# Gate and up projections of two swiglus: seven products of halves for 18 of 22 pairs, with the second projection's rows between them

## The reference

```python
def swiglu(x, w_in, w_out):
    gate, up = jnp.split(x @ w_in, 2, axis=-1)
    return (jax.nn.silu(gate) * up) @ w_out
```

## Time and profile before

| | |
|---|---|
| runs, median | 1790.06 us (1788.73 to 1791.06) |
| the profiled execution, its own time | 1788.67 us |
| its span | 1786.9 us |
| granted TensorE clock, mean | 0.998 |
| matmuls | 8634 |
| busy, DVE / ACT / POOL | 879.1 / 676.5 / 9.0 us |
| loaded and stored | 176.85 MB, 99 GB/s |

### The profile page before, as it was taken

How to read it: one execution, slowest core, us unless ns; L and a number is a source line. 1 busy time by engine, 2 the same in 40 slices (tenths; PEclk the granted TensorE clock), 3 DMA queues, 4 the chain that set the end, 5 groups by cost and what they waited for, 6 DMA issues and landing times.

```text
span 1786.9 us, 21356 instructions
## 1 busy us (share of the span) xinstructions
PE 1771.8 (99%) x8634; PEld 1450.8 (81%) x8634; DVE 879.1 (49%) x1440; ACT 676.5 (38%) x1129; POOL 9.0 (1%) x36
## 2 busy tenths in 40 slices
PE   9999999999999999999999999999999999999998
PEld 8777778888888897666888888888888898888887
DVE  4688783333333734555833332338436762434344
ACT  4467633222223234565332231232545552323141
POOL 0000000000000000000000000000000000000000
PEclk9999999999999999999999999999999999999999
DMA  8232223323333342322233333352323333232321
GB/s 289 85 100 85 85 82 98 114 83 95 106 94 106 107 130 72 94 83 60 83 101 100 94 111 83 101 152 76 94 60 103 98 107 106 85 104 94 100 90 47
DMA packets 218180, 176.85 MB, mean 99 GB/s; under 512 B 9010, under 2 KB 177875, under 8 KB 218083
## 3 DMA queue, kind: packets, MB, share of 16 engines
q1 hardware_dynamic: 218082, 175.49, 32.6%
HBM read 173.32 MB, written 7.38 MB: 101 GB/s over the span
## 4 chain that ended last, share of the span: by engine, by line
PE 96%; DVE 3%; DMA 0%; ACT 0%; issue 0%; SPq 0%; DVEq 0%; ACTq 0%
PE ps L577 29%; PE ps L579 29%; PE ps L578 29%; PE ps L857 2%; PE ps L899 1%; PE ps L923 1%; PE ps L911 1%; PE ps L877 1%; PE ps L782 1%; PE ps L867 0%; DVE small L1465 0%; DMA raw<-in_a_w_qkv 0%; DVE xl L1385 0%; DVE x L1527 0%; DVE x L1461 0%; PE ps L887 0%
## 5 line engine op out<-in xcount | busy, mean ns | idle before, releaser
L577 PE MATMUL ps<-xh,whi 128*128 128x512 f32 (+1 forms) x1176 | 442.8, 377 | 0.3 <-DVE xl L1385 0.3
L579 PE MATMUL ps<-xh,wlo 128*128 128x512 f32 (+1 forms) x1176 | 431.6, 367 | 0.0
L578 PE MATMUL ps<-xl,whi 128*128 128x512 f32 (+1 forms) x1176 | 431.1, 367 | 0.0
L1372 DVE TENSOR_TENSOR wlo<-raw,whi 128x1024 fp32r<-128x1024 f32 x235 | 283.4, 1224 | 241.0 <-ACT whi L1067 240.3
L1067 ACT ACTIVATE whi<-raw 128x1024 fp32r<-128x1024 f32 x235 | 243.7, 1050 | 109.9 <-PE ps L579 79.3
L577 PEld LDWEIGHTS ps<-xh,whi 128*128 128x128 f32 x1176 | 222.4, 189 | 46.1 <-issue 10.2
L577 PE MATMUL ps<-whi,hh 128*128 128x512 f32 x648 | 256.8, 396 | 0.8 <-ACT arena L1249 0.8
L579 PE MATMUL ps<-whi,hl 128*128 128x512 f32 x648 | 252.5, 390 | 0.0
L578 PE MATMUL ps<-wlo,hh 128*128 128x512 f32 x648 | 252.2, 389 | 0.0
L579 PEld LDWEIGHTS ps<-xh,wlo 128*128 128x128 f32 x1176 | 222.3, 189 | 36.8
L578 PEld LDWEIGHTS ps<-xl,whi 128*128 128x128 f32 x1176 | 222.5, 189 | 35.8 <-issue 1.2
(11 more groups left out here) (204 smaller groups left out, 2040.9 us busy)
## 6 DMA issues: line engine op xcount, KB each, us to landing
raw<-in_ffn_w_in SPq DMA_DIRECT2D x88, 512.0 KB, 4.1
raw<-in_w_ff SPq DMA_DIRECT2D x64, 512.0 KB, 4.1
raw<-in_ffn_w_out SPq DMA_DIRECT2D x44, 512.0 KB, 3.8
raw<-in_a_w_qkv SPq DMA_DIRECT2D x23, 512.0 KB, 5.0
raw<-in_w_in SPq DMA_DIRECT2D x20, 512.0 KB, 3.8
raw<-in_kv_w SPq DMA_DIRECT2D x16, 512.0 KB, 4.3
bias_skewed<-bias_rows SPq DMA_DIRECT2D x8, 640.0 KB
raw<-in_a_w_o SPq DMA_DIRECT2D x8, 512.0 KB, 4.4
```

Source lines behind the costliest of these rows:

```text
L577: e.matmul(o, ah, bh, start=start, stop=False)
L578: e.matmul(o, ah, bl, start=False, stop=False)
L579: return e.matmul(o, al, bh, start=False, stop=stop)
L1372: e.tensor_tensor(lo, self.raw[:, m % RAW, :], f32(hi), ALU.subtract).then_inc(s.lo, 1)
```

## The change

The first 4 blocks of each swiglu stay as they are. For the other 18, the 1024 features and the 512 tokens are cut into halves, and gate and up are the two halves of the output. Instead of eight products of a half (4 feature blocks, 256 tokens), seven are made, from sums of the weights' halves and of the tokens' halves (Strassen's scheme in Winograd's form). A product is 4 x 3 matmuls of 256 columns.

- Weights: of a pair's two tiles, four unit tiles are made, x1 (up as it is, products 1 and 2), x2 (both sums s2 and s1, products 6 and 5), s4 (half a tile, product 3) and x3 (s3 and the second half of gate, products 7 and 4). DVE makes the four sums of 128 x 512 (`sums`); units are split as tiles are, and SP reloads a raw slot behind the split of s4 or x3.
- Tokens: behind norms 1 and 3 ACT also copies the unrounded tokens out of PSUM (`x_raw`), and during the four plain pairs DVE makes four sums of 128 x 1024, each of which is split.
- Results: products 1, 6, 7 and 4 add up in one PSUM bank, and ACT copies out the state after 1, 6 and 7 (`keep`); 2 stands alone in a second bank, which 5 and 3 then take. DVE adds copies and second bank (`combine`, `hidden`), ACT's silu is in two halves of 256 (`gates`).
- Order: `PIECES` says, for each pair, which of four places between its seven products take a piece of the second projection's rows. There are 56 such pieces, those of blocks 0 to 13; the rows of the last 8 blocks stay at the norm's edge. The groups are 4, 4, 4, 2 and 8 blocks, so DVE adds to `x` 40 times instead of 24.
- Splits run 3 units ahead in the pairs, with one after each product.
- Some semaphores of small loads are merged, so that their users wait for all loads of a set: `a_in` stands for those of the first attention (cosines, sines, masks, gains), `mix_in` counts 112 instead of 80 and takes in the mixer's norm vectors. SP loads norm 4's vectors, and POOL clears the mixer's small tiles, only after the last low part of the second swiglu's hidden blocks.

```diff
-FFN_GROUPS = [(0, 6), (6, 8), (14, 8)]
...
+FFN_GROUPS = [(0, 4), (4, 4), (8, 4), (12, 2), (14, 8)]
+PLAIN = 4
...
+AHEAD_PAIRS = 3
+PUMP = 1
+PIECES = "1011 1011 1011 1011 1011 1111 1111 1111 1111 1111 1111 1111 1111 1011 0101 0101 0101 0101 0000".split()
...
+    def sum_next(self):
+
+        n = self.n_split
+        if n > self.summed and n < len(self.kinds) and self.kinds[n] == "s2":
+            for i in range(3):
+                self.step("sums", n + i)
+            self.summed = n + 2
...
+        if norm in (1, 3) and t == 3:
+            self.t_steps = [("t_sum", 1), ("t_sum", 2), ("t_sum", 3), ("t_split", 1), ("t_sum", 4), ("t_split", 4),
+                            ("t_split", 3), ("t_split", 2)]
...
+    def product(self, pair, j):
+        if self.unfinished:
+            self.step("hidden_low", self.unfinished.pop())
+        name, f = f"ffn_w_in{pair.layer}", pair.f
+        if j == 1:
+            pair.bank1 = self.bank(hold=True)
+            x1 = self.take("cols", name, FF + f * 128, frees=False)
+            pair.units[1], pair.units[2] = (x1, 0), (x1, 1)
+            pair.up = len(self.tiles) - 1
+        elif j == 2:
+            pair.bank2 = self.bank(hold=True)
+        elif j == 6:
+            self.tiles.append(("cols", name, f * 128))
+            pair.gate = len(self.tiles) - 1
+            x2 = self.unit("s2", pair, None)
+            pair.units[6], pair.units[5] = (x2, 0), (x2, 1)
+            pair.units[3] = self.unit("s4", pair, pair.up), 0
+            x3 = self.unit("s3", pair, pair.gate)
+            pair.units[7], pair.units[4] = (x3, 0), (x3, 1)
+        value = pair.done[j] = self.count("product") + 1
+        self.step("product", pair, j)
+        if j in (1, 6, 7):
+            pair.copied[j] = self.count("copied") + 1
+            pair.free[j] = self.read.get((j, pair.buf if j == 6 else 0), 0)
+            self.step("keep", pair, j)
+        if j in (2, 7, 3):
+            pair.combined[j] = self.count("combined") + 1
+            self.read[{2: (1, 0), 7: (7, 0), 3: (6, pair.buf)}[j]] = pair.combined[j]
+            if j != 3:
+                self.step("combine", pair, j, self.counts["h"] - (j == 7))
+        if j in (2, 5, 4, 3):
+            self.done(pair.units[j][0], "product", value)
+        if j == 4:
+            self.release(pair.bank1)
+            pair.gates = self.count("gates") + 1
+            self.step("gates", pair, self.counts["h"])
+        if j == 3:
+            self.release(pair.bank2)
+            pair.hidden = self.block(pair.block)
+            self.count("combined")
+            self.step("hidden", pair)
+            self.unfinished.append(pair)
+        if not self.by_hand:
+            self.pump(PUMP)
+
+    def some_t(self, n):
+
+        for _ in range(min(n, len(self.t_steps))):
+            what, i = self.t_steps.pop(0)
+            if what == "t_sum":
...
+        self.unfinished, self.t_steps = [], []
+        wanted = []
...
+        self.some_t(8)
+        rows = [self.rows("res", (f"ffn_w_out{layer}", 0), f0, nf, norm=norm if f0 == 14 else None, group=g)
+                for g, (f0, nf) in enumerate(FFN_GROUPS)]
+        pieces = itertools.chain(*rows[:-1])
+        pairs = {f: Pair(layer, f) for f in range(PLAIN, 22)}
+        self.ahead = AHEAD_PAIRS
+        for j in (1, 2):
+            self.product(pairs[PLAIN], j)
+        for f in range(PLAIN, 23):
+            here, last, following = pairs.get(f), pairs.get(f - 1), pairs.get(f + 1)
+            n = PIECES[f - PLAIN]
+            for pair, j in ((here, 6), ("rows", 0), (last, 4), (last, 3), ("rows", 1), (here, 5), (following, 1),
+                            ("rows", 2), (here, 7), (following, 2), ("rows", 3)):
+                if pair == "rows":
+                    self.some(pieces, int(n[j]))
+                elif pair:
+                    self.product(pair, j)
+        self.ahead = AHEAD
+        self.step("hidden_low", self.unfinished.pop())
+        assert next(pieces, None) is None
+        self.ffn_blocks[layer] = self.counts["h"]
...
+        self.run(rows[-1])
...
+            elif what == "product":
+                pair, j = arg
+                unit, half = pair.units[j]
+                wh, wl = (part.rearrange("p (k c) -> p k c", k=8) for part in self.parts(unit))
+                w.wait_ge(s.lo, unit + 1)
+                w.wait_ge(s.xl, x_at + 8)
+                if j in (1, 2, 3):
+                    c, k0 = slice(256, 512) if j == 3 else slice(0, 256), 0 if j == 1 else 4
+                    th, tl = (v[:, k0:k0 + 4, c] for v in (xh, xl))
+                else:
+                    w.wait_ge(s.t_lo, t_at + {5: 1, 4: 2, 7: 3, 6: 4}[j])
+                    th, tl = self.t[{4: 4, 5: 1, 6: 2, 7: 3}[j]]
+                b = pair.bank1 if j in (1, 6, 7, 4) else pair.bank2
+                if j in (1, 2):
+                    w.wait_ge(*freed[b])
+                elif j in (5, 3):
+                    w.wait_ge(s.combined, pair.combined[2 if j == 5 else 7])
+                else:
+                    w.wait_ge(s.copied, pair.copied[{6: 1, 7: 6, 4: 7}[j]])
+                for k in range(4):
+                    m = mm3(e, ps[b][:, 0:256], wh[:, 4 * half + k, :], wl[:, 4 * half + k, :], th[:, k, :],
+                            tl[:, k, :], j in (1, 2, 5) and k == 0, k == 3, skip_group_check=True)
+                m.then_inc(s.product, 1)
...
+                w.wait_ge(s.product, pair.done[j])
+                if pair.free[j]:
+                    w.wait_ge(s.combined, pair.free[j])
+                e.activation(dst, ps[pair.bank1][:, 0:256], ACT.Copy).then_inc(s.copied, 1)
+
+            elif what == "gates":
+                pair, blocks = arg
+                w.wait_ge(s.product, pair.done[4])
+                w.wait_ge(s.hl, blocks - 1)
+                e.activation(self.silu_out[pair.buf][:, 0:256], ps[pair.bank1][:, 0:256], ACT.Silu).then_inc(s.act, 1)
+                own += 1
+                w.wait_ge(s.combined, pair.combined[7])
+                out = self.silu_out[pair.buf][:, 256:512]
+                e.activation(out, out, ACT.Silu).then_inc(s.gates, 1)
+
+            elif what == "hidden":
+                pair, = arg
+                w.wait_ge(s.combined, pair.combined[3] + 1)
+                e.activation(self.hh[:, pair.block, :], self.h_out[pair.buf], ACT.Copy).then_inc(s.hh, 1)
+
+            elif what == "t_split":
+                i, n = arg
+                w.wait_ge(s.t_raw, n if i == 1 else (n + 3) // 4 * 4)
+                if i == 2:
...
+                    if norm in (1, 3):
+                        e.activation(self.x_raw[:, half * 4:half * 4 + 4, t * 128:t * 128 + 128],
+                                     ps[b][:].rearrange("p (k c) -> p k c", k=4), ACT.Copy).then_inc(s.x_raw, 1)
...
+                kind, pair, _ = self.plan.units[m]
+                up, gate = self.raw[:, pair.up % RAW, :], self.raw[:, pair.gate % RAW, :]
+                s2, s1 = self.s21[:, 0:512], self.s21[:, 512:1024]
+                if kind == "s2":
+                    if self.sums_at[m] > 2:
+                        w.wait_ge(s.sums, self.sums_at[m] - 2)
+                        w.wait_ge(s.lo, last_s2 + 1)
+                    last_s2 = m
+                    w.wait_ge(s.raw[pair.up % RAW], self.raw_at[pair.up])
+                    w.wait_ge(s.raw[pair.gate % RAW], self.raw_at[pair.gate])
+                    e.tensor_tensor(s1, gate[:, 0:512], gate[:, 512:1024], ALU.add).then_inc(s.sums, 1)
+                    w.wait_ge(s.sums, self.sums_at[m] - 1)
+                    e.tensor_tensor(s2, s1, up[:, 0:512], ALU.subtract).then_inc(s.sums, 1)
+                elif kind == "s4":
+                    w.wait_ge(s.lo, pair.units[1][0] + 1)
+                    w.wait_ge(s.sums, self.sums_at[pair.units[6][0]])
+                    e.tensor_tensor(up[:, 512:1024], up[:, 512:1024], s2, ALU.subtract).then_inc(s.sums, 1)
+                else:
+                    w.wait_ge(s.sums, self.sums_at[pair.units[6][0]] - 1)
+                    e.tensor_tensor(gate[:, 0:512], up[:, 0:512], gate[:, 0:512], ALU.subtract).then_inc(s.sums, 1)
+
+            elif what == "combine":
+                pair, j, blocks = arg
+                kept = self.part if j == 2 else self.three
+                w.wait_ge(s.hl, blocks)
+                dst = self.h_out[pair.buf][:, 0:256] if j == 2 else self.silu_out[pair.buf][:, 256:512]
+                w.wait_ge(s.copied, pair.copied[1 if j == 2 else 7])
...
+                e.tensor_tensor(dst, kept, ps[pair.bank2][:, 0:256], ALU.add).then_inc(s.combined, 1)
+
+            elif what == "hidden":
+                pair, = arg
+                h, n = self.h_out[pair.buf], pair.combined[3]
+                w.wait_ge(s.copied, pair.copied[6])
+                w.wait_ge(s.product, pair.done[3])
+                e.tensor_tensor(h[:, 256:512], self.two[pair.buf], ps[pair.bank2][:, 0:256],
+                                ALU.add).then_inc(s.combined, 1)
```

(23 more changed lines are left out.)

215 lines of the change are left out of this document (143 added, 72 removed).

## The result

The changed kernel took 1766.86 us (median of 4 runs, 1766.08 to 1768.23), the kernel before in the same rounds 1790.28 us (1788.73 to 1791.06). The ratio is 0.9871, with a 95% interval of 0.9854 to 0.9888: 23.4 us faster. The forecast of 1763.9 us was 3.0 us low. The profiled execution took 1768.23 us, with a span of 1766.4 us at a mean granted clock of 0.996.

What follows compares the result with a forecast made beforehand. The prediction took PE's matmuls to bound the kernel: -28.8 + 2.0 + 0.6 = -26.2 us, from 1790.06 to 1763.9 us, with its own range 1761 to 1770 and 1760 to 1777 for 8 in 10.

Steps and rivals of the forecast that it cites:

- PE, -28.8: Gate and up products: a pair falls from 10.88 to 10.08 us, 0.80 saved in each of 36 pairs, 28.8 us.
- rows are the same matmuls in another order: Second projection's pieces between products: 56 x 6 matmuls at an unchanged 0.2267 us, 76.2 us per swiglu.
- Inside the pairs, 0: PE waits on copies, additions, sums and splits within the pairs: all covered by other products, so 0 us.
- the walk through the queues: DVE's and ACT's queues through one round: DVE falls behind up to 0.8 us per narrow round with a row tile.
- The last pair, +2.0: After the 21st pair's product 7, PE waits for the copy and perhaps DVE: 1.0 us each, +2.0 for both.
- The edges, +0.6: Norms 1 and 3, where ACT first copies unrounded tokens: 0.3 us each, bounds 0 and 1.1, +0.6 for both.
- Token sums, DMA, SP and POOL, 0: Token sums covered by four plain pairs; loads, slot reuse, merged semaphores and POOL's clearing stay ahead of users: all 0.
- A few rounds leak: Rival: four narrow rounds and two more lose 1 us in each swiglu, +12, 1776 us; chance 0.15.
- DVE with ACT becomes the bound: Rival: DVE and ACT wait in turn around silus and hidden low part; pair 15.3 us, +36 us, 1800; chance 0.08.
- An issue cost of waits: Rival: the fixed part belongs to semaphore waits, not matmuls; 0.03 us per product, 15 us, 1779; chance 0.05.
- The smaller gap is paid: Rival: matmuls cost columns / 2.4 plus 2.5 ns, so 36 pairs give 43 us, 1750 us; chance 0.01.
- The change does not do what it says: Rival: the seven products' matmuls are not at 0.120 us; 0.1295 would equal before; taken as no change, chance 0.03.

Runs made afterwards that it cites:

- the repetition: The changed kernel measured again with no edit, for a second profile: 1765.36 us beside 1790.76 for the kernel before, ratio 0.9862.
- the run with 19 pairs: Three plain blocks in each swiglu instead of four, against the changed kernel with some row pieces moved to avoid PE waits: 1766.82 us, ratio 0.9873.
- the one with five additions: The changed kernel with five extra DVE additions of 128 x 512 per pair, each waited for, before the hidden block's low part: 1810.37 us, ratio 1.0119.
- the run with halves: The kernel before with gate and up of 18 pairs per swiglu as 96 matmuls of 256 columns, not 48 of 512: 1812.31 us, ratio 1.0122.
- the run with plain pairs: The changed kernel with no seven products, all pairs plain, but the new copies, token sums, groups and additions kept: 1797.02 us, ratio 1.0037.

## Why the prediction was right, point by point

- **PE, -28.8.** The spacing held at 0.120 in the products, and the fixed part of 13.3 ns, measured by itself, is 13.4. A nineteenth pair gave 0.80 us in swiglu 1. What the term left out is the turn between 512 and 256 columns: 56 pieces a swiglu cost 1.14 us, **+2.3**. The step that failed is "rows are the same matmuls in another order": the order has a price. None of the rows I had read shows such a turn.
- **Inside the pairs, 0.** Right for products: no sum, split or combination of theirs made PE wait in any pair but the last. Wrong for the rows between them: the walk through the queues looked at what products wait for, not at the low part of a row tile, which stood in DVE's queue behind the work of a round. 0.57 + 0.30 a swiglu, **+1.7**.
- **The last pair, +2.0.** 0.74 each, **+1.5**, at the copy as named, between the nearest row's 0.6 and the 1.0 taken. Product 3 did not wait.
- **The edges, +0.6.** 0: from the first to the last token block of norm 3 it takes 21.96 us in the kernel before and in the repetition. The waits on `xl` behind the norms were 0.6 and 0.9 us in the two profiles, and 0.8 before.
- **DVE.** 1109 us busy where 1130 was forecast, ACT 787 where 795. The mean durations were right (0.418, 0.69, 1.22), but instructions that follow each other overlap: two low parts take 2.36 us together, not 2.44. The windows of the changed kernel from 312 to 566 us, nearly all rounds of swiglu 1, sum to:

```profile
sum 254.00, PE 253.18 PEld 238.17 DVE 195.94 ACT 113.80 POOL 0.00; mean PE 63.29 PEld 59.54 DVE 48.99 ACT 28.45 POOL 0.00
```

That is 77%, or 11.0 us of 14.3 a pair, not 11.9. ACT has 6.4, not 6.9.
- **Token sums, DMA, SP and POOL, 0.** No wait in PE's list names them.
- **Sum.** -28.8 + 2.3 + 1.7 + 1.5 = -23.3 us, against -26.2 forecast: the same mechanism, with two terms of 4.0 us together that had been taken as 0. That the forecast missed by only 3 us is in part luck: 1.1 us too much had been taken for the last pair and the edges. The medians of the three measurements of the changed kernel lie 23.4, 25.4 and 24.2 under the kernel before in their rounds.
- **Rivals.** "A few rounds leak" foresaw 12 us in the narrow rounds; what leaked is 3.2 us, at row tiles and the last copy, and nothing in the narrow rounds. "DVE with ACT becomes the bound" did not happen in this kernel, but the run with 19 pairs (3.0 us) and the one with five additions (45 us) show it close by. What stood there on the clock, 1 us more for each wait of over 2 us, did not come each time: behind the 2.99 us with 19 pairs the granted clock stayed 1.00, and with five additions it fell behind four of 14 waits of over 1.7 us. "An issue cost of waits" is refuted: the products' borders have no gap, one product between pieces takes 1.432 us and four take 5.752. "The smaller gap is paid" and "The change does not do what it says" are refuted by the spacing of 0.120.

## What to carry to other kernels

Seven products of halves give what the spacing of the smaller matmul leaves of the eighth: work it out from start to start at both widths, not from the columns. Cover for another engine's new work is counted in its busy time per round: it held at 91% here and no longer at 98%; what is late first is not the new work but what shares its queue, here the operands of rows. Where two widths of matmul alternate, larger bunches save the turns, here 1.0 us of 1764.

## What had not been expected of the hardware

- A turn from 256 to 512 columns and back costs about 0.02 us, without a wait: a run of 512-column matmuls takes 0.028 us more than its count times 0.2267, whether it has six, twelve or, in the run with halves, 192, and the run of 256-column ones beside it 0.008 less than its count times 0.120. Why is open.
- The granted clock falls behind the same waits in some executions and not in others. After PE had waited 2.3 us, in the run with plain pairs, PE ran six matmuls at the upper level (three in swiglu 2) and the granted clock was 0.50 for the next 3.4 us. After two waits of 0.98 and 0.88 us at norm 3 it fell so in three of the eleven profiled executions with seven products, and not in the other eight, whose waits there are the same. Behind the wait at the start it fell in three of the eleven, not all of them the same ones. What decides that is open.
- The wait at the start of the kernel was between 0.7 and 2.1 us in these executions, with the same instructions ahead of it.
